# Nine places for the experts' weights, later bias, norm and gate rows, and a loop of three pairs

## The reference, cut to what matters

```
x = first_block(x, ...)    # hybrid_mixer; layer_norm; moe; layer_norm(ln2)
    # moe, per expert e:
    hcat = xblk @ w_up[e] + b_up[e]          # 1024 x 2048, 8 MB
    act  = x_glu * sigmoid(1.702 * x_glu) * (x_lin + 1)
    y    = act @ w_down[e] + b_down[e]       # 1024 x 1024, 4 MB
return second_block(x, ...)
    # mod = silu(c) @ w_ada + b_ada; g1, g2 are two of its six parts
    # h = ada_norm(x); proj = h @ w_in; neighbourhood attention adds bias from na_rpb
    # x = x + g1 * (mixed @ w_out); x = x + g2 * (mlp)
```

## Time and profile before

| | |
|---|---|
| median of 3 runs | 1542.79 us (1540.13 to 1542.86) |
| profiled execution: span, first to last instruction | 1539.3 us |
| busy: PE / DVE / ACT / POOL | 93% / 38% / 29% / 2% |
| TensorE clock granted, mean | 0.998 of full |
| DMA queue of SP | 515.24 MB, 84.4% of 16 engines' span |
| expert chunks, issue to landing | 32.0 to 35.3 us, 2 MB each |

### The profile page before, as it was taken

How to read it: one execution, slowest core, us unless ns; L and a number is a source line. 1 busy time by engine, 2 the same in 40 slices (tenths; PEclk the granted TensorE clock), 3 DMA queues, 4 the chain that set the end, 5 groups by cost and what they waited for, 6 DMA issues and landing times. The chain is left out here.

```text
span 1539.3 us, 19789 instructions
## 1 busy us (share of the span) xinstructions
PE 1428.0 (93%) x7981; PEld 842.8 (55%) x7981; DVE 592.5 (38%) x1032; ACT 448.3 (29%) x580; POOL 38.1 (2%) x79
## 2 busy tenths in 40 slices
PE   7999999999999998988989989989889999899998
PEld 7988798344344433423423333333333788778887
DVE  4985447211210210210210210210211686777765
ACT  4654543221121111111111111111121545454343
POOL 1000030000000000000000000000000022000000
PEclk9999999999999999999999999999999999999999
DMA  8598998999999999999999999999999251245552
GB/s 262 166 309 261 327 329 289 427 428 427 429 428 428 429 428 428 429 428 429 427 429 429 428 429 428 428 429 429 428 428 404 87 185 63 83 162 190 187 192 90
DMA packets 130687, 516.98 MB, mean 336 GB/s; under 512 B 11173, under 2 KB 99086, under 8 KB 106030
## 3 DMA queue, kind: packets, MB, share of 16 engines
q1 hardware_dynamic: 130350, 515.24, 84.4%
q10 hardware_dynamic: 288, 1.05, 0.2%
HBM read 515.22 MB, written 1.05 MB: 335 GB/s over the span
## 5 line engine op out<-in xcount | busy, mean ns | idle before, releaser
L1254 PE MATMUL ps<-ring,xg 128*64 128x512 f32 x1536 | 340.8, 595 | 29.9 <-DMA ring<-in_expert_w_up 24.3
L1382 DVE TENSOR_TENSOR glu<-ps,bupT 128x512 f32<-128x512 f32 x32 | 22.1, 691 | 722.6 <-PE ps L1263 722.6
L1254 PEld LDWEIGHTS ps<-ring,xg 128*64 128x64 f32 x1536 | 108.5, 137 | 259.1 <-issue 202.9
L80 ACT ACTIVATE hrow<-ps 128x1024 f32<-128x1024 f32 x32 | 32.8, 1024 | 479.0 <-PE ps L1254 479.0
L1278 PE MATMUL ps<-ring,act 128*64 128x512 f32 x768 | 170.8, 596 | 0.0
L1254 PE MATMUL ps<-more,xg 128*64 128x512 f32 x512 | 114.2, 594 | 14.4 <-DMA more<-in_expert_w_up 14.4
L2058 PE MATMUL ps<-h_halves,w_hi 128*128 128x512 f32 x352 | 122.2, 394 | 1.1 <-DVE h_halves L2211 1.1
L1278 PEld LDWEIGHTS ps<-ring,act 128*64 128x64 f32 x768 | 52.0, 137 | 100.5 <-issue 89.7
L2160 DVE TENSOR_TENSOR w_lo<-ring,w_hi 128x2048 fp32r<-128x2048 f32 x36 | 82.5, 2291 | 60.2 <-ACT w_hi L80 60.2
L2060 PE MATMUL ps<-h_halves,w_lo 128*128 128x256 f32 x352 | 97.5, 277 | 0.0
L80 ACT ACTIVATE y<-ps 64x512 f32<-64x512 f32 x64 | 37.9, 592 | 179.1 <-PE ps L1278 178.7
(11 more groups left out here) (411 smaller groups left out, 2158.9 us busy)
## 6 DMA issues: line engine op xcount, KB each, us to landing
ring<-in_expert_w_up SPq DMA_DIRECT2D x96, 2048.0 KB, 32.0
ring<-in_expert_w_down SPq DMA_DIRECT2D x48, 2048.0 KB, 35.3
more<-in_expert_w_up SPq DMA_DIRECT2D x32, 2048.0 KB, 32.7
more<-in_expert_w_down SPq DMA_DIRECT2D x16, 2048.0 KB, 35.3
ring<-in_w_in SPq DMA_DIRECT2D x30, 1024.0 KB, 8.2
ring<-in_w_ada SPq DMA_DIRECT2D x24, 1024.0 KB, 5.7
ring<-in_w_gu SPq DMA_DIRECT2D x22, 1024.0 KB, 5.1
ring<-in_w_down SPq DMA_DIRECT2D x11, 1024.0 KB, 4.9
```

Source lines behind the costliest of these rows:

```text
L80: return nc.scalar.activation(out, x, ACT.Copy)
L1254: last = nc.tensor.matmul(up[a2 * CAP:(a2 + 1) * CAP, u, :], k.xg[:, q, h * CAP:(h + 1) * CAP], w[:, c:c + 512], start=(q == 0), stop=(q = ...
L1382: link(nc.vector.tensor_tensor(k.glu[:, :, :, :], g, b[:, 0].to_broadcast(wide), ALU.add))
```

## The change

- **Nine places.** Chunk i goes to place i mod 9. The ninth (`EXTRA`, place 5) is the SBUF of `xT` and `xn`, which with `x` become one tensor `wide`. Seven chunks (0, 1, 2, 6, 5, 3, 4) are issued in `branches`, chunks 7 and 8 at the start of `experts`.
- **Bias and norm rows.** `bm_loads` and `late_loads` target what is now the ninth place, so both are issued after its last use: behind four of the five w_in chunks, and ahead of the fifth, whose slot is now 7.
- **Gate rows.** The diagonals are written by ACT early in `experts`; PE's ones-matmuls take the place of the five fillers at the start of `second_mix`; ACT copies them between its squares, where it wrote two high halves of w_in before. Those two move behind the halves of h.
- **Loops.** PE's loop is five turns of three pairs and one pair outside (before, eight of two). ACT's has 15 pairs and one outside. In the last pair the gather is split in two halves, one between the last two down chunks and one behind them, and ACT takes the gathered rows after the expert's output.

```diff
-LATE = [7, 8, 9, 10, 11]
+LATE = [8, 9, 10, 11, 7]
-PLACES = 8
-GROUP = 4 * CHUNKS
+PLACES = 9
+PLACE_SLOT = {0: 6, 1: 0, 2: 2, 3: 8, 4: 10, 6: 4}
+EXTRA, MORE = 5, 7
+LOOPED = 3
@@ branches, SP
             load_expert(k, sp, a, 0, 0)
             sp.wait_ge(k.w_low1, S_OUT)
-            load_expert(k, sp, a, 0, 3)
+            load_expert(k, sp, a, 0, 1)
             sp.wait_ge(k.first_used, PE_BRANCH + 2)
-            load_expert(k, sp, a, 0, 4)
+            load_expert(k, sp, a, 0, 2)
             sp.wait_ge(merged, 2)
-            load_expert(k, sp, a, 0, 5)
-            for dst, src in k.bm_loads:
-                sp.dma_start(dst, src).then_inc(k.bm_in, 16)
+            load_expert(k, sp, a, 0, 6)
+            sp.wait_ge(k.x_low, X_M + 1)
+            load_expert(k, sp, a, 0, EXTRA)
             for c in (1, 2):
                 sp.wait_ge(k.w_low1, S_OUT + 4 * c)
-                load_expert(k, sp, a, 0, c)
+                load_expert(k, sp, a, 0, 2 + c)
@@ experts, SP, behind the last expert chunk
-            for dst, src in k.late_loads:
-                sp.dma_start(dst, src).then_inc(k.ln_in, 16)
             for i, slot in enumerate(LATE):
+                if i == len(LATE) - 1:
+                    sp.wait_ge(used, done + place_free(EXTRA))
+                    for dst, at in k.late_loads:
+                        sp.dma_start(dst, at).then_inc(k.ln_in, 16)
+                    for dst, at in k.bm_loads:
+                        sp.dma_start(dst, at).then_inc(k.bm_in, 16)
                 src, kt, cols = k.last[i]
-                sp.wait_ge(used, done + (E * PER + q + 1 - 2 * PLACES))
+                sp.wait_ge(used, done + slot_free(slot))
                 sp.dma_start(slot_last(k, i, kt, cols), src).then_inc(k.last_in[i], 16)
@@ experts, PE
+                if tail:
+                    down_weights(r, turn, at, n, 1, (0,))
+                    gather(nc, k, 3, range(KD // 2))
+                    down_weights(r, turn, at, n, 1, (1,))
+                    gather(nc, k, 3, range(KD // 2, KD)).then_inc(g_done, 1)
@@ second_mix, PE
-            fill(nc, k, 4, k.gB[:, 0, 0:512], 5)
+            pe.wait_ge(k.gd, 1)
+            for b in range(4):
+                nc.tensor.matmul(k.ps[:, 4 + b, :], k.ones[:, :], k.diag[b // 2][:, (b % 2) * 512:(b % 2 + 1) * 512],
+                                 start=True, stop=True).then_inc(gb_done, 1)
             for t in range(TT):
                 pe.wait_ge(xn_ready, t + 1)
+                pe.wait_ge(gb_out, t + 1)
@@ second_mix, ACT, for each t behind its square and root
-                high(t + 1)
+                act.wait_ge(gb_done, 2 * t + 2)
+                act_copy(nc, k.gB[:, t, :], k.flat[:, (2 + t) * 1024:(3 + t) * 1024]).then_inc(gb_out, 1)
@@ second_mix, ACT, behind the high halves of h
+            high(1)
+            high(2)
             evacuate(0)
@@ program
-        k.x, k.xT = sb("x_gates", [P, TT, D]), sb("xT_bias", [P, KD, T])
+        k.wide = sb("x_xT_xn", [P, 3 * TT * D])
```

More of the change, by code:

```diff
@@ L834, in choose, with gather @@
     return last
-def gather(nc, k):
-    for q in range(KD):
-        out = k.flat[:, 5 * 512 + q * P:5 * 512 + (q + 1) * P]
+def gather(nc, k, bank, tiles):
+    for q in tiles:
+        out = k.flat[:, bank * 512 + q * P:bank * 512 + (q + 1) * P]
         for t in range(TT):
@@ L1242, in _, with up_weights @@
             pe.wait_ge(hot_ready, 1)
-            gather(nc, k).then_inc(g_done, 1)
+            gather(nc, k, 5, range(KD)).then_inc(g_done, 1)
             extra = extra_rounds(pe)
             pe.wait_ge(k.bias_in, 32)
-            def up_weights(group, two, n, h):
+            def up_weights(r, turn, at, n, h):
                 for q in range(KD):
                     if q % 2 == 0:
-                        chunk = expert_arrived(k, pe, group, 2 * two * CHUNKS + h * UP_CHUNKS + q // 2)
+                        chunk = expert_arrived(k, pe, r, turn, at * PAIR + h * UP_CHUNKS + q // 2)
                     w = chunk[:, (q % 2) * 2048:(q % 2 + 1) * 2048]
@@ L1265, in units_turned, with down_weights @@
                 last.then_inc(hT_done, 1)
[L1267 to L1270, removed]
+            def down_weights(r, turn, at, n, h, halves=(0, 1)):
+                if 0 in halves:
+                    pe.wait_ge(act_ready, n * 2 + h + 1)
+                    pe.wait_ge(y_ready, n * 2 + h + 1)
+                for j in (2 * v + w for v in halves for w in range(2)):
                     if j % 2 == 0:
-                        chunk = expert_arrived(k, pe, group, 2 * two * CHUNKS + 2 * UP_CHUNKS + 2 * h + j // 2)
+                        chunk = expert_arrived(k, pe, r, turn, at * PAIR + 2 * UP_CHUNKS + 2 * h + j // 2)
                     w = chunk[:, (j % 2) * 2048:(j % 2 + 1) * 2048]
@@ L1281, in down_weights, with pair @@
                     last.then_inc(used, 1)
-            def pair(group, two, n):
+            def pair(r, turn, at, n, tail):
                 pe.wait_ge(xg_ready, n + 1)
-                up_weights(group, two, n, 0)
+                up_weights(r, turn, at, n, 0)
                 pe.wait_ge(acc_done, n * 2 + 2)
@@ L1301, in pair @@
                 pe.wait_ge(hot_ready, n + 2)
[L1302 to L1308, removed]
+                if tail:
[3 more added lines that the diff above has]
+                    gather(nc, k, 3, range(KD // 2, KD)).then_inc(g_done, 1)
+                else:
+                    pe.wait_ge(acc_done, n * 2 + 4)
+                    gather(nc, k, 5, range(KD)).then_inc(g_done, 1)
+                    down_weights(r, turn, at, n, 1)
+            with pe.Fori(0, extra + 1) as r:
+                with pe.Fori(0, TURNS) as g:
+                    for at in range(LOOPED):
+                        pair(r, g, at, r * PAIRS + g * LOOPED + at, False)
+                pair(r, TURNS, 0, r * PAIRS + (PAIRS - 1), True)
             pe.wait_ge(selT_ready, extra * pairs + pairs + 1)
             pe.wait_ge(y_ready, extra * (2 * pairs) + 2 * pairs + 1)
+            pe.wait_ge(acc_done, extra * (2 * pairs) + 2 * pairs + 2)
             scatter()
@@ L1321, in _, with out_rows, gathered, pair @@
             nc.scalar.activation(k.trig[:, :, :], k.ang[:, :, :], ACT.Sin).then_inc(k.trig_ready, 1)
[L1322 to L1329, removed]
+            for n, row in enumerate((GATE1, GATE2)):
+                for m in range(KD):
+                    ins = nc.scalar.activation(k.diag[n][:, m * P:(m + 1) * P], k.ident[:, :], ACT.Copy,
+                                               scale=k.mod[:, row + m:row + m + 1])
+            ins.then_inc(k.gd, 1)
+            def out_rows(n, h):
+                act.wait_ge(used, n * 24 + 20 + 4 * h)
+                for a2 in range(2):
+                    ins = act_copy(nc, k.y[h * CAP:(h + 1) * CAP, a2 * 512:(a2 + 1) * 512],
+                                   down[a2 * CAP:(a2 + 1) * CAP, :])
+                ins.then_inc(y_ready, 1)
+            def gathered(n, src):
+                act.wait_ge(g_done, n + 2)
+                act_copy(nc, k.xg[:, :, :].rearrange("p k n -> p (k n)"), flat(src)).then_inc(xg_ready, 1)
+            def pair(n, tail):
                 for h in range(2):
@@ L1336, in _ @@
                         .then_inc(sig_ready, 1)
-                out_rows(0)
+                out_rows(n, 0)
                 act.wait_ge(selps_done, n + 1)
                 act_copy(nc, k.selT[:, :], seT).then_inc(selT_ready, 1)
-                act.wait_ge(g_done, n + 2)
-                act_copy(nc, k.xg[:, :, :].rearrange("p k n -> p (k n)"), flat(rows)).then_inc(xg_ready, 1)
-                out_rows(1)
+                if not tail:
+                    gathered(n, rows)
+                out_rows(n, 1)
+                if tail:
+                    gathered(n, turned)
+            with act.Fori(0, extra + 1) as r:
+                with act.Fori(0, PAIRS - 1) as p:
+                    pair(r * PAIRS + p, False)
+                pair(r * PAIRS + (PAIRS - 1), True)
         @blk.vector
```

72 lines of the change are left out of this document (36 added, 36 removed).

## The result

The changed kernel takes **1555.74 us** (median of 4 runs, 1553.35 to 1556.68), the kernel before 1542.82 us (4 runs beside it, 1540.13 to 1543.95): ratio **1.0086, 95% interval 1.0074 to 1.0098**, 12.9 us slower. Measured again later: 1556.04 us and 1.0086 [1.0073, 1.0099]. The direction and the late bias were forecast. The size was not: 1549.8 was said, and 1555.74 lies above the range.

A forecast was written before the change was run, and what follows sets the result against it. Expert stage bound by DMA at 428 GB/s; -4.9 and -1.3 us gained, but PE waits for a late bias: first projection +7.0 us, gains included. Span 1539.3 + 7.0 = 1546.3, median 3.5 above: 1549.8 us; range 1541 to 1553.5.

The forecast's parts named there:

- Ninth chunk: Expert stream: nine chunks instead of eight in or on their way at loop start, so it ends one chunk earlier, -4.90 us.
- Gate rows out of branches: In `branches`, PE loses two groups of 1.96 us; taken as 0 because DVE's chain sets the pace, up to -0.9.
- the stream starts at the same time: Start of `experts`: expert stream begins no earlier or later, since its last two chunks still wait for the stage.
- Loops of three pairs: PE's expert loop: fewer branches, 4.6 us slack per steady pair, so 0; a possible fetch in the last pair is hidden.
- Split gather: Last expert pair: half the gather fills PE's 1.29 us wait for y, so the scatter starts 1.3 us earlier.
- Bias late: Experts' end: bias starts at 1189.1 us behind w_in, takes 12.2, lands at 1201.3; projection +7.0 us; chance 0.60.
- both rates (3.0 and 7.6 us): Rivals for the bias load: w_in's rate, 1539.0 us, chance 0.17; full-queue rate, 1543.6 to 1545.3 us, chance 0.18.
- the estimate by Anatomy of one DMA: Bias load: 2.0 us plus bytes at 436 GB/s per DMA, estimated 4.4 us in all, bias in at 1193.5.
- Norm rows hidden: Start of `second_mix`: DVE can start its norm about 2 us after the stage's end, hidden by the later bias.
- From bias to projection: In `second_mix`: 12.7 us of flips, copies, squares and turn from bias to first projection, plus 1.7 for a low clock.
- Nothing behind the projection: After the first projection nothing changes: ACT's two later high halves and the late fifth w_in chunk are covered, 0.

The follow-up runs named there:

- e1: Changed kernel with two filler matmuls of 512 columns in each of the two places of `branches` where gate matmuls stood; 1554.06 us, ratio 1.0071.
- g1: Kernel before with only the gate rows moved as in the change, eight places and bias still loaded in `branches`; 1545.71 us, ratio 1.0020.
- f1: Changed kernel with e1's fillers, norm rows behind the first w_in chunk, bias loaded in `second_mix` and flipped before the fifth projection; 1540.93 us, ratio 0.9989.
- e3: Changed kernel with the bias loads and fifth w_in chunk issued first thing in `second_mix` instead of in the experts' stage; 1558.39 us, ratio 1.0095.
- e2: Changed kernel without the 16 bias loads and PE's wait for them, bias left out of the computation; 1544.52 us, ratio 1.0011.
- after_again: The changed kernel measured once more, unaltered, on the same chip; 1556.04 us, ratio 1.0086.
- e4: Kernel before, eight places and gate rows in `branches`, with only bias and norm rows issued behind four of five w_in chunks; 1556.51 us, ratio 1.0088.
- f2: Changed kernel with e1's fillers, bias and norm rows ahead of w_in, three w_in chunks moved to `second_mix`; 1540.16 us, ratio 0.9991, later 1540.97 us.
- h1: f2 with four filler matmuls on PE ahead of its wait for the bias in `second_mix`; 1539.18 us, ratio 0.9975.
- h2: Kernel before, eight places, with only f2's order of bias and norm rows, w_in and high halves; 1543.40 us, ratio 1.0006.

## Why the prediction was wrong, step by step

- **Ninth chunk, -4.90.** Right in size. First up weights to last DMA wait: 871.05 us before, 866.29 after, -4.76; in every kernel with nine places 865.4 to 866.7, with eight 870.6 to 871.3.
- **Gate rows out of branches, taken as 0, bounds -0.9 to 0. This is the step that failed.** I priced the four ones-matmuls of the earlier trace rows by their own 2 x 1.96 us and asked only what they delay. They also filled PE between tile turns: without them PE stands 0.76 and 0.79 us between the turns, and the clock is 0.50 for 13.7 us from 260.4 us on. All behind it to the stage's start runs slower: gather 4.96 instead of 4.01 us, up weights 4.3 us late. That shift goes through the whole DMA-bound stage, because its last two chunks wait for the stage to start ("the stream starts at the same time" fell with it): the queue is empty from about 262 us, and 0 GB/s move until SP's issue at 272.28. e1 takes the low clock and the late start away, g1 (+3.1 us, 1.7 to 4.5) has them alone. I had used this very reasoning on PE's idle time at the other end and not here.
- **Loops of three pairs, 0.** Right as far as seen: the stretch at 428 GB/s is unchanged. It was not run by itself.
- **Split gather, -1.3.** Wrong, without effect on the sum. Last DMA wait to scatter: 45.48 us before, 45.75 after, 45.7 to 45.9 in all with the split but f1 (46.2), and 45.5 in all without. PE's 1.29 us before the scatter is gone, but there is a new wait of 1.12 us for the same ACT copy before the down weights at 1179.03, which the whole gather had covered, and two halves take 4.3 us against 3.93.
- **Bias late.** Right in mechanism and nearly in size. Forecast 1201.3 us, that is 995.9 from w_out; measured 1000.6: +4.7, of which 4.3 are the shifted start. The duration from the old row, taken as 12.2 us, was right, and both rates (3.0 and 7.6 us) were not: the 16 issues take SP 12.63 us, and the median DMA lands 5.3 us behind its issue.

```profile
x_xT_xn<-in_na_rpb SPq DMA_DIRECT2D x16, 64.0 KB, 5.3
```

 Of the two statements from the Trainium skill (DMA: Bandwidth & Descriptors), the estimate by Anatomy of one DMA, 4.4 us, was far too short: in e3, into a nearly empty queue, it is 16.2 us from SP's first bias issue (1193.13) to the end of PE's wait (1209.32). That section fits single DMAs issued by GpSimd, and here SP issues sixteen. With Specifications, where line rate wants 512 B or more, the 138 GB/s of before at a share of 1.17 agrees. The 124 GB/s of after while the bias moves, at a share of 0.65, can't decide it, since there SP's issues may set the pace.
- **Norm rows hidden.** Right here, but only under the bias; e2 shows 1.95 us of DVE waiting for them.
- **From bias to projection, 12.7 + 1.7.** 14.31 us measured, low clock included (0.50 from 1199.1 us for 13.7 us, longer than charged; the flips take 5.85 instead of 3.67 us). Two sums in the prediction are off by a little: its terms here add up to 12.6, and from 243 to 257.1 us it is 14.1, not 13.9.
- **Nothing behind the projection.** Wrong by a small term. Span less first projection is 330.6 us before and 332.2 after, +1.5, and all of it arises in one place, at the start of `output`. In both kernels the clock falls to 0.50 for 3.4 us there, but not at the same point. Before, it falls on six filler matmuls ahead of a wait and costs nothing: the first matmul with w_out stands 112.4 us behind the projection, and 112.5 after. After, it falls on the matmuls with the first w_out chunk, and PE needs 14.15 us from their start to the second chunk's instead of 12.66. Before, then after:

```profile
1313.59 4.51 PE L850 MATMUL ps<-x_gates,ident 128*128 128x512 f32 x6 [1.50 <-PEq L1441]
1313.60:1317.60 4.00, 4.00 (x6) 1.70 (x7) 3.48 (x6) 3.88 (x5) 0.00 (x0) 0.57 0.00 0
```

```profile
1335.60:1339.60 4.00, 4.00 (x24) 4.00 (x23) 4.00 (x7) 1.21 (x3) 0.00 (x0) 0.57 0.01 2
```

 after_again and e3 have the drop where after has it; before, g1 and e2 have it on the fillers; e1, e4, f2, h1 and h2 have none there. What decides this is open. In the other traces the remainder lies between 330.8 and 335.3 us (f1, with the flips inside). Part of that is the MLP's up projection, 121.8 us in before and after but 124.1 in e1, g1, e3 and e4, with the granted clock at 1.00 in all of them; why is open too.

The sum from w_out: +7.0 forecast, +4.3 clock in `branches`, +0.4 the rest of the bias' landing: +11.7 at the projection, and +1.5 behind it, +13.2 in the trace against +12.9 in the medians. The 4.3 is read from landmarks in traces; by itself in time (g1) the term is 3.1 us. It is the largest of the missed terms, but not the whole gap: e1, without it, still takes 1554.06 us where 1549.8 was forecast.

## What to carry to other kernels

A matmul that is removed because it is off the path may be what keeps TensorE busy between two waits. Look at the gaps that open without it, most of all ahead of a long DMA-bound stage whose start then shifts as a whole, and put fillers there first. A load of many short-run DMAs is priced by its old issue-to-landing rows, not by bytes; here it cost least when it was issued ahead of the next bulk load (f2) or into an idle queue (f1), so that the first instruction of a stage did not wait long for it.

## What the runs showed of the hardware

- Gaps of only 0.76 and 0.79 us, in a stretch with PE busy for 3.44 of 5 us, went with a fall of the granted clock from 1.00 to 0.50, which then held for 13.7 us, with PE busy for 9.89 us of the 12 from 262 to 274 us. In before and e1, with 1.96 us of matmuls in each of two places there, it stayed at 1.00.
- A clock of 0.50 for 3.4 us at the start of `output` cost nothing where it fell on fillers ahead of a wait (before) and 1.5 us where it fell on matmuls without slack (after, after_again).
- SP's time to issue the same 16 DMAs of 64 KB: 10.6 us (e3) and 11.4 us (f1) with little or nothing in the queue, 12.6 to 13.4 us behind w_in (after, e4), 29.1 and 41.3 us (f2, h2) behind expert chunks. Even with a free queue that is 0.66 to 0.71 us for each, 92 to 99 GB/s: with the engines' share at 0.65 this points to SP's issue, not the engines, as the pace; it was not run by itself.
- While SP issues, a stage does not end: DVE and ACT stood at the block's end until SP was done (8.59 and 12.16 us in after), a wait that shows in the profile as one for PE's queue. With those issues moved into the next stage (e3) DVE starts its norm at 1194.65 us.
